# Mixture-of-experts block: gate by one ScalarE function, expert rows added up by the scatter, bias added on TensorE

## What is computed

```python
top_vals, top_idx = lax.top_k(h @ w_router + b_router, 4)      # 4 of 32 experts a token
weights = softmax(top_vals)
# for each expert e, for the tokens that chose it:
gu = x @ w_gate_up[e] + b_gate_up[e]                           # 1024 -> 2048
gate, up = split(gu, 2)
gate = minimum(gate, 7.0)
up = clip(up, -7.0, 7.0)
act = (up + 1.0) * (gate * sigmoid(1.702 * gate))
yb = act @ w_down[e] + b_down[e]                               # 1024 -> 1024
y = segment_sum(yb * weight, token)                            # 4 rows added per token
x = x + gate2 * y
out = rmsnorm(x)
```

## Time and profile before

| | before |
|---|---|
| median of 3 runs | 3197.2 us |
| the profiled execution | 3199.73 us, of it 3198.2 us span |
| PE / DVE / ACT / POOL busy | 85% / 64% / 48% / 8% |
| route phase | about 1093 to 1187 us |
| experts phase | about 1187 to 3099 us |
| combine phase | about 3104 to 3198 us |

### The profile page before, as it was taken

One profiled execution on the slowest core, in us unless ns is written; L12 is line 12 of the kernel. 1 busy time (PEld: TensorE's weight loads), 2 busy tenths in 40 slices (PEclk: granted clock), 3 DMA queues, 4 the chain that ended last, 5 costly groups with the idle time before them and its releaser, 6 DMA issues. The chain is left out here.

```text
span 3198.2 us, 42791 instructions
## 1 busy us (share of the span) xinstructions
PE 2709.4 (85%) x12364; PEld 2128.5 (67%) x12365; DVE 2038.1 (64%) x3092; ACT 1532.5 (48%) x2203; POOL 271.1 (8%) x366
## 2 busy tenths in 40 slices
PE   1499979896789617999999999999999999999972
PEld 1388857674667516777777777777777777777750
DVE  6511034444553327867777896798678979787948
ACT  1212134342341106746555775587456757575721
POOL 0000011100000041111010111011001100010100
PEclk8699989997899758999999999999999999999985
DMA  8422132211342308957668896699668969886957
GB/s 338 168 102 76 47 101 80 70 50 56 104 148 97 133 28 274 357 209 247 225 233 295 300 367 225 235 367 346 211 210 280 368 223 367 292 301 231 356 194 262
DMA packets 450243, 685.50 MB, mean 214 GB/s; under 512 B 27473, under 2 KB 368865, under 8 KB 445825
## 3 DMA queue, kind: packets, MB, share of 16 engines
q1 hardware_dynamic: 420000, 591.83, 54.0%
q0 software_dynamic: 27872, 84.41, 7.3%
q10 hardware_dynamic: 2304, 8.39, 0.7%
HBM read 633.85 MB, written 59.60 MB: 217 GB/s over the span
## 5 line engine op out<-in xcount | busy, mean ns | idle before, releaser
L2034 DVE TENSOR_TENSOR e_gu_lo<-gu_raw,e_gu_hi 128x1024 fp32r<-128x1024 f32 x564 | 680.0, 1219 | 162.7 <-ACT e_gu_hi L1916 162.7
L78 PE MATMUL e_pgu<-e_gu_hi,e_x_hi 128*128 128x512 f32 x1568 | 643.3, 410 | 6.0 <-issue 6.0
L1916 ACT ACTIVATE e_gu_hi<-gu_raw 128x1024 fp32r<-128x1024 f32 x564 | 574.9, 1047 | 105.8 <-SPq L1740 82.9
L79 PE MATMUL e_pgu<-e_gu_lo,e_x_hi 128*128 128x512 f32 x1568 | 620.2, 396 | 0.0
L80 PE MATMUL e_pgu<-e_gu_hi,e_x_lo 128*128 128x512 f32 x1568 | 620.0, 395 | 0.0
L80 PEld LDWEIGHTS e_pgu<-e_gu_hi,e_x_lo 128*128 128x128 f32 x1568 | 294.9, 188 | 71.9
L78 PE MATMUL e_pdn<-e_dn_hi,e_a_hi 128*128 128x512 f32 x784 | 317.3, 405 | 26.0 <-DVE e_a_lo L2068 26.0
L78 PEld LDWEIGHTS e_pgu<-e_gu_hi,e_x_hi 128*128 128x128 f32 x1568 | 295.4, 188 | 65.9 <-issue 6.4
L2040 DVE TENSOR_TENSOR e_dn_lo<-dn_raw,e_dn_hi 128x1024 fp32r<-128x1024 f32 x280 | 333.0, 1219 | 4.5 <-ACT e_dn_hi L1922 4.4
L79 PEld LDWEIGHTS e_pgu<-e_gu_lo,e_x_hi 128*128 128x128 f32 x1568 | 295.9, 189 | 59.1
L80 PE MATMUL e_pdn<-e_dn_hi,e_a_lo 128*128 128x512 f32 x784 | 310.2, 396 | 0.0
(11 more groups left out here) (340 smaller groups left out, 4145.5 us busy)
## 6 DMA issues: line engine op xcount, KB each, us to landing
gu_raw<-in_w_gate_up_dram SPq DMA_DIRECT2D x572, 512.0 KB, 10.0
dn_raw<-in_w_down_dram SPq DMA_DIRECT2D x142, 1024.0 KB, 10.0
gu_bias<-in_b_gate_up_dram SPq DMA_DIRECT2D x141, 256.0 KB, 9.3
wada<-in_w_ada_dram SPq DMA_DIRECT2D x24, 1024.0 KB
c_y<-expert_rows SPq DMA_DIRECT2D x8, 2048.0 KB
win_raw<-in_w_in_dram POOLq DMA_DIRECT2D x6, 2048.0 KB, 8.8
proj_by_token<-out_stage SPq DMA_DIRECT2D x32, 256.0 KB, 2.0
wg_raw<-in_w_in_dram POOLq DMA_DIRECT2D x16, 512.0 KB, 4.8
```

The source lines that it names most:

```text
L78: pe.matmul(out, a[0], w[0], start=first, stop=False)
L79: pe.matmul(out, a[0], w[1], start=False, stop=False)
L1916: act.activation(gu_hi[:, b, 2 * j:2 * j + 2], gu_raw[:, b, 2 * j:2 * j + 2].rearrange("p k g n -> p k (g n)"), ACT.Copy).then_inc(gu_hi_d ...
L2034: dve.tensor_tensor(gu_lo[:, b, 2 * j:2 * j + 2], gu_raw[:, b, 2 * j:2 * j + 2].rearrange("p k g n -> p k (g n)"), gu_hi[:, b, 2 * j:2 * j ...
```

## The change

Route: entries of the lists have three words (row for the gather, row for the scatter, weight). Unused entries hold 8191 for the gather, which is now bounded, a row of 128 spare ones for the scatter, and weight 0. `y_sum` in DRAM is set to zero by nine 512 KB DMAs. The biases are loaded once as a [128, 1024] table, 1 is added to the up half, its fp32r part and rest are stored as `bias_hl`, and the table with the 1 goes back to DRAM for `load_bias`. A row `pick_of` says for each round which expert it is.

```diff
+            for j in range(4):
+                sp.dma_start(braw[j * NE:(j + 1) * NE], m.b_gate_up[0, :, (j // 2) * FF:(j // 2 + 1) * FF]).then_inc(bias_raw, 16)
...
+            sp.wait_ge(zeroed, 1)
+            for t in range(NT + 1):
+                sp.dma_start(m.y_sum[t * P:(t + 1) * P, :], zero[:]).then_inc(zero_out, 16)
...
+            dve.memset(zero[:], 0.0).then_inc(zeroed, 1)
+            v.step(dve.memset(m.pick[:].bitcast(F32), 0.0))
+            dve.wait_ge(bias_raw, 64)
+            dve.tensor_scalar(braw[2 * NE:P], braw[2 * NE:P], 1.0, None, ALU.add).then_inc(bias_up, 1)
             dve.wait_ge(pool_set, 9)
```

```diff
+        def by_pe(two, c):
+            return not two or c == 0
...
-                        if k == (FIRST_K if l else 3):
+                        if k == (TURN_A_K if l else 3):
...
+                        if k == KT // 2 and by_pe(two, c):
+                            if l == 0:
+                                pe.wait_ge(picked, 2 * r + 2)
+                            for g in range(2):
+                                ins = pe.matmul(p_gu[:, l % 2, g], pick[:, g], m.bias_hl[:, c * FC:(c + 1) * FC], start=False, stop=False)
```

`TURN_A_K` is 5. SyncE issues `load_bias` only in double rounds, for chunks 1 to 3. ScalarE and VectorE:

```diff
-            def sigmoid(n):
-                act.wait_ge(clamped, n + 1)
-                act.activation(sg[:], gb[:, 0], ACT.Sigmoid, scale=ALPHA).then_inc(sigm, 1)
+            def swish(n, parity, on_pe):
+                if on_pe:
+                    act.wait_ge(hidden, n + 3)
+                    act.wait_ge(activated, n + 1)
+                    act.activation(sg[:], p_gu[:, parity, 0], ACT.Gelu_apprx_sigmoid).then_inc(swished, 1)
+                else:
+                    act.wait_ge(with_bias, n + 3)
+                    act.activation(sg[:], gb[:, 0], ACT.Gelu_apprx_sigmoid).then_inc(swished, 1)
...
-                dve.tensor_scalar(gb[:, 0], gb[:, 0], LIMIT, None, ALU.min).then_inc(clamped, 1)
-                dve.tensor_scalar(gb[:, 1], gb[:, 1], -LIMIT, LIMIT, ALU.max, ALU.min).then_inc(up_clamped, 1)
+                dve.tensor_scalar(gb[:, 1], gb[:, 1], 1.0 - LIMIT, 1.0 + LIMIT, ALU.max, ALU.min).then_inc(up_clamped, 1)
...
+            def activate(n, parity, on_pe):
+                dve.wait_ge(swished, n + 1)
+                if on_pe:
+                    dve.tensor_scalar(gb[:, 1], p_gu[:, parity, 1], 1.0 - LIMIT, 1.0 + LIMIT, ALU.max, ALU.min).then_inc(up_clamped, 1)
+                    dve.sem_inc(with_bias, 1)
+                dve.wait_ge(up_clamped, n + 3)
+                dve.scalar_tensor_tensor(out=av[:], in0=sg[:], scalar=GATE_MAX, in1=gb[:, 1], op0=ALU.min, op1=ALU.mult).then_inc(activated, 1)
```

GpSimd and the evacuation:

```diff
-                                        in_offset=bass.IndirectOffsetOnAxis(ap=rows[:, s, 0:1].bitcast(U32), axis=0)).then_inc(gathered[s], 16)
+                                        in_offset=bass.IndirectOffsetOnAxis(ap=rows[:, s, 0:1].bitcast(U32), axis=0),
+                                        bounds_check=SEQ - 1, oob_is_err=False).then_inc(gathered[s], 16)
...
-                pool.indirect_dma_start(out=m.y4[:, :], out_offset=bass.IndirectOffsetOnAxis(ap=dest[:, 0, s:s + 1].bitcast(U32), axis=0),
-                                        in_=ys[:], in_offset=None, bounds_check=SEQ * TOPK - 1, oob_is_err=False).then_inc(scattered, 16)
+                pool.indirect_dma_start(out=m.y_sum[:, :], out_offset=bass.IndirectOffsetOnAxis(ap=dest[:, 0, s, 0:1].bitcast(U32), axis=0),
+                                        in_=ys[:], in_offset=None, compute_op=ALU.add).then_inc(scattered, 16)
...
-                act.activation(ys[:], p_dn[:, s], ACT.Copy).then_inc(y_out, 1)
+                act.wait_ge(dest_kept, kept)
+                act.activation(ys[:], p_dn[:, s], ACT.Copy, scale=dest[:, 0, s, 1:2].bitcast(F32)).then_inc(y_out, 1)
```

So gathers fetch only the rows in use, and scatters write all 128 rows of a block, adding to what is there. Combine loads one row per token (0.5 MB a tile) and adds it once:

```diff
-                for k in range(TOPK):
-                    if k:
-                        dve.wait_ge(weighed, TOPK * t + k)
-                    dve.scalar_tensor_tensor(out=acc[:, b], in0=y[:, b, k], scalar=m.wtop[:, t, k:k + 1], in1=acc[:, b] if k else ps[:, b],
-                                             op0=ALU.mult, op1=ALU.add).then_inc(weighed, 1)
+                dve.tensor_tensor(acc[:, b], y[:, b], ps[:, b], ALU.add).then_inc(summed, 1)
```

More of the change, by code:

```diff
@@ L38 @@
 NO_ROW = 8191
+LIST_WORDS = 3
 CH = 4
@@ L1539, in _ @@
                 v.inc(dve.tensor_scalar(m.wtop[:, t], sh[:, t], tot[:, t:t + 1], None, ALU.mult))
+            v.wait()
+            v.step(dve.tensor_copy(entry[:, :, :, 2].bitcast(F32), m.wtop[:].rearrange("p t k -> p k t")))
             dve.wait_ge(counted, 1)
@@ L1750, in body @@
                 for c in range(CH):
-                    wait_apart(sp, with_bias, U + c * (1 + two) + 2)
-                    bs(here if c < 3 else there, (c + 1) % CH, (c + 1) % 2)
+                    if two and c < CH - 1:
+                        wait_apart(sp, with_bias, U + 2 * c + 2)
+                        bs(here, c + 1, (c + 1) % 2)
                     for half in range(2):
@@ L1760, in body @@
                     dn(here if c < 2 else there, (c + 2) % CH, c % 2)
-            rounds(sp, body)
-            n = sp.value_load(m.rounds[0:1, 0:1], min_val=1, max_val=MAX_ROUNDS)
+                if not two:
+                    sp.sem_inc(bias_in[0], 16)
+                    sp.sem_inc(bias_in[1], 32)
+            total, n = rounds(sp, body)
             for half in range(2):
@@ L1799, in _ @@
                 wait_apart(pool, gathered[s], 16)
-            pool.tensor_copy(dest[:, 1], rows[:, :, 1]).then_inc(dest_kept, 1)
+            pool.tensor_copy(dest[:, 1], rows[:, :, 1:3]).then_inc(dest_kept, 1)
             wait_apart(pool, dest_kept, 1)
@@ L2069, in low_a, with choose @@
                                   ALU.subtract).then_inc(a_lo_done, 1)
+            def choose(r):
+                for g in range(2):
+                    rows_ = slice(g * 2 * NE, (g + 1) * 2 * NE)
+                    dve.tensor_copy(pick[rows_, g], m.pick_of[rows_, bass.ds(r, 1)].to_broadcast([2 * NE, P])).then_inc(picked, 1)
             dve.sem_inc(with_bias, 2)
+            dve.sem_inc(up_clamped, 2)
+            dve.sem_inc(activated, 1)
             dve.sem_inc(a_lo_done, 1)
+            choose(0)
             for j in range(QG):
@@ L2095, in piece @@
                                 gu_piece(16 * r + QG * (c + 1) + j, c + 1, j)
-                    if l:
-                        with_biases(n - 1, pc, (l - 1) % 2, 32 * r + 16 * (pc // 2) + 16)
+                    if l and not by_pe(two, pc):
+                        with_biases(n - 1, pc, (l - 1) % 2, r)
                     piece()
                     if l:
-                        activate(n - 1)
+                        activate(n - 1, (l - 1) % 2, by_pe(two, pc))
                         piece()
@@ L2107, in body @@
                         low_x(r + 1, 0)
-                        with_biases(n, c, l % 2, 32 * r + 32)
+                        if not by_pe(two, c):
+                            with_biases(n, c, l % 2, r)
                         low_x(r + 1, 1)
-                        activate(n)
+                        activate(n, l % 2, by_pe(two, c))
+                        dve.wait_ge(pick_used, r + 1)
+                        choose(r + 1)
                     while todo:
```

121 lines of the change are left out of this document (77 added, 44 removed).

## The result

The kernel after takes 3125.8 us (median of 4 runs, 3124.0 to 3128.2), before it 3195.5 us: a ratio of 0.978, interval 0.9768 to 0.9791. The forecast was 3117 us in a range of 3085 to 3168. The profiled execution took 3128.2 us with a span of 3126.6, 71.5 us less than that of before. The number is near, in part by luck: two of the terms behind it are not, and they err to opposite sides.

A forecast was written before the change was run, and what follows sets the result against it. The prediction took TensorE to bound double rounds and DMA single ones, with VectorE close behind. Its terms, -59 + 8 - 34.5 + 2.5 + 1.5 = -81.5 us, took 3199.7 to 3118, given as 3117 us, range 3085 to 3168.

The forecast's parts named there:

- Single rounds, -59 forecast: Experts phase, 21 single rounds: each falls from 41.1 to 38.3 us, -2.8 a round, -59 us in all.
- So DMA is the first bound of single rounds: Single rounds before the change: DMA share 1.08 of 41.1 us, with VectorE close behind at 38.8.
- I get `e_act` ready 1 to 3 us before TensorE asks: Single rounds: the activation comes in time, except in a round's second unit, where TensorE waits 0.4 to 0.5 us.
- VectorE ... is no bound: Single rounds: VectorE's work falls from 38.8 to 34.8 us, so it does not limit the round.
- single rounds hardly move: Rival: raw-weight waits grow or D is about 5; singles -15 us, whole 3162 us, chance 0.10.
- D: DMA time of one adding scatter of 128 rows in a single round: taken as 2.7 us, between 1.34 and 7.0.
- the one with a late `e_act`: Rival, TensorE pays in full: dear bias matmuls, earlier transpose waits 1 us a round; singles -32, whole 3154 us, chance 0.15.
- DMA's own term: Single rounds: the DMA bound is 35.7 + 0.93 D, so 38.2 us a round with D at 2.7.
- TensorE's term: Bias matmuls of 256 columns at 0.12 us each: +1.0 us a single round, +0.5 a double one.
- Double rounds, +8 forecast: Experts phase, 14 double rounds: TensorE's bias in chunk 0 and `choose` add 0.6 us a round, +8 us.
- Combine, -34.5 forecast: Combine phase: fewer adds save 4.0 us a tile, -32 us over 8 tiles, and an earlier first tile -2.6.
- Route, +2.5 forecast: Route phase: masks come 2 us later behind VectorE's first steps, small copies add 0.5; +2.5 us (0 to 6).

The follow-up runs named there:

- a_plain: The kernel after with scatters that overwrite rows in place of adding to them: 3120.1 us, ratio 0.9765.
- a_oldplace: The kernel after with its SBUF tiles put back where they stand in the kernel before: 3148.1 us, ratio 0.9849.
- a_no_pe: The kernel after with every bias added on VectorE from pieces loaded in every chunk, none by TensorE: 3140.4 us, ratio 0.9828.
- b_layout: The kernel before with only the order of small SBUF tiles changed, so all stationary tiles start at a multiple of 128 bytes: 3184.1 us, ratio 0.9962.
- a_gap64: The kernel after with an unused tile of 64 bytes a partition ahead of `e_a_hi`, moving the down product's stationary tiles: 3135.9 us, ratio 0.9815.

## Why the prediction was right and wrong

- **Single rounds, -59 forecast, -18.5 measured.** This is the step that failed, in two sentences of it. "So DMA is the first bound of single rounds" took a share above 1 and ScalarE's wait for weights for a bound; with 11 to 16% less DMA in single rounds, both kernels keep their time. And "I get `e_act` ready 1 to 3 us before TensorE asks": VectorE's 3.9 us less work turned into 3.2 us more idle time, 2.2 of it in front of `e_x_lo`, since I followed the activation's chain through VectorE's order and not the next input's; TensorE still waits 2.1 us a round for `e_act`. "VectorE ... is no bound" compared its work with the round, and left out the waits that an order fixes. The rival "single rounds hardly move" had named the place (-15 us) at a chance of 0.10; its reasons did not hold: the waits for raw weights did not grow but went from these rounds, and D is not 5. What does explain the small gain, VectorE waiting for ScalarE's `e_x_hi`, stood in no rival; nearest was the one with a late `e_act`, 1 us a round (chance 0.15), 2.1 measured. By its own sign (single rounds above 39.5) the prediction's account is wrong here.
- **DMA's own term was right.** With D = 2.7 it gave 38.2 us a round; D came out at 2.6 (1.34, the prediction's own price of a plain scatter, and 1.25 measured by a_plain), and with the order mended the later single rounds of a row take up to 39.4 us with full loads and 36.9 to 37.0 with half of `w_down`. The Trainium skill (Collectives: The Full Stack, "The bandwidth ceiling") has two source reads for one write; a_plain agrees with the doubled cost, and shows no second read.
- **TensorE's term was a little too dear.** A double round with the old place of tiles has 71.8 us (a_oldplace) and 72.0 in the kernel before; a_no_pe against after puts the bias of one chunk at 0.3 us, 0.07 a matmul, where 0.12 was taken.
- **Double rounds, +8 forecast, -15.9 measured.** The terms were too dear by some 0.5 us a round; the larger part, 17 us, is the place of tiles in SBUF, which the prediction did not look at. It hid part of the miss in single rounds, and that is luck: without it the change would have taken 3148 us, inside the range and 31 us above the forecast.
- **Combine, -34.5 forecast, -37.3 measured.** Right in place and in size: a tile takes 5.1 and not 5.5 us, because all but one of the waits for loads went too; the first tile came 2.4 us earlier, 2.6 forecast.
- **Route, +2.5 forecast, -2.6 measured.** The masks do come later, at 1110.70 after 1109.48, and x's first transposes earlier, at 1200.74 after 1203.34. But the end of this phase differs by up to 9 us between executions of the same phase, so neither the forecast nor the -2.6 can be told from no change.
- **The last adding scatter, +1.5 forecast, +2.7 measured** (2.1 and 0.6). Of its signs, "ScalarE's evacuation waits for a scatter" was to prove the prediction wrong: it does so once, for 9.5 us, and nowhere else.
- **35 table loads**: as forecast.

## What to carry to other kernels

Before an engine is called free of the critical path, look in its order of time at where it stands idle: if ready work stands behind the instruction that waits, less work on the engine can turn into more waiting, until that work is put ahead of it. Work plus idle time fills the period for every engine, so only moving the work tells. A full DMA queue is no bound by itself (leave out a part of its bytes and look). A removed load and add that bring 15 us may bring 64 once the order behind them is mended, so mend the order before judging the part, and compare the granted clock of the rounds before putting a difference down to the edit. Look where a small new tile moves the ones that TensorE reads.

## What was not expected of the hardware

A stationary tile that begins 64 bytes behind a multiple of 128 bytes in its partition makes each fp32r matmul of 512 columns 233 ns and not 227, at the same clock: 1.2 to 1.3 us per double round (b_layout, a_oldplace), 22 us of the kernel after (a_oldplace), 12 of the kernel before, where the clock took some back (b_layout), and by product in a_gap64. Six nanoseconds a matmul less went with longer single rounds in b_layout, not shorter ones: TensorE waited 1.9 to 2.0 us for `e_act` and not 1.8, and in nine of them its clock then stood at half for 3.4 us. The DMA share stood at 1.08 in rounds of 41.1 us that didn't depend on DMA and at 1.07 to 1.08 in rounds of 37.6 and 37.7 us that came near to it, so a share above 1 does not tell by itself how near DMA is to being the bound.
